# A two-block sequence-mixing kernel on one core: the convolution branch moved to the front of the first block, its taps placed behind the matrix LSTM's projection, and the modulation rows computed in array quadrants

## The reference, cut to what matters

```python
mod_x = split(silu(c) @ w_ada + b_ada, 6);  mod_c = split(silu(c_ctx) @ w_ada + b_ada, 6)
h  = rmsnorm(x, g_norm1) * (1 + mod_x[1]) + mod_x[0]
hc = rmsnorm(ctx, g_norm1) * (1 + mod_c[1]) + mod_c[0]
u_rw, u_cv, u_ml, u_gate = split(h @ w_in)          # RWKV, convolution, matrix LSTM, three merge gates
ya = rwkv_mixer(u_rw, hc @ w_in[rw]); yc = mlstm_mixer(u_ml, hc @ w_in[ml])
a, g = split(u_cv); z = a * sigmoid(g)              # 512 channels each
z = depthwise_conv(z, cv_dw, cv_db)                 # 31 taps, within rows of 64 tokens
yb = silu(layernorm(z, cv_lnw, cv_lnb))
m = sig(ga) * (ya @ p_a) + sig(gb) * (yb @ p_b) + sig(gc) * (yc @ p_c)
x = x + mod_x[2] * (m @ w_out)
x = x + mod_x[5] * mlp(rmsnorm(x, g_norm2) * (1 + mod_x[4]) + mod_x[3])
```

## Time and profile before

| what | value |
|---|---|
| median of 3 runs | 4786.41 us (4783.46 to 4788.29) |
| profiled execution | 4790.0 us, its span 4788.2 us |
| TensorE busy | 4233.6 us (88%) |
| VectorE, ScalarE, GpSimd busy | 2180.8 (46%), 1340.5 (28%), 156.6 us (3%) |
| TensorE's mean granted clock | 0.914 |
| matrix LSTM projection, start to end | 89.8 to 232.4 us |
| RWKV output, from the first slab load | 1029.4 to 1098.4 us |
| convolution projection | 1098.4 to 1146.6 us |
| merge | 1146.6 to 1446.4 us |

### The profile page before, as it was taken

The page is one execution under the profiler, slowest core; times in us unless marked ns, Lnnn a source line. Parts: engine busy times, 40 slices in busy tenths (PEclk is TensorE's granted clock), DMA queues, the critical chain, the costliest instruction groups (busy, mean ns, idle before and its releaser), DMA issues.

```text
span 4788.2 us, 69852 instructions
## 1 busy us (share of the span) xinstructions
PE 4233.6 (88%) x30212; PEld 3338.8 (70%) x30212; DVE 2180.8 (46%) x2940; ACT 1340.5 (28%) x1886; POOL 156.6 (3%) x194
## 2 busy tenths in 40 slices
PE   6987878878677999999987989998999987989998
PEld 3855768856455787788666667887788666567886
DVE  2135467753744444433636344334333636444334
ACT  3133233312122232322221342222222321342222
POOL 0000012120000000000001000000000001000000
PEclk8878979989889999999978989999999978999999
DMA  5101000033123323233200113232333200112331
GB/s 191 45 1 44 9 2 3 3 110 105 53 71 109 117 96 105 80 93 93 71 28 16 40 39 89 85 106 86 95 94 91 63 19 15 40 53 80 97 100 54
DMA packets 319059, 322.10 MB, mean 67 GB/s; under 512 B 10032, under 2 KB 243552, under 8 KB 317984
## 3 DMA queue, kind: packets, MB, share of 16 engines
q1 hardware_dynamic: 312144, 287.53, 19.5%
q0 software_dynamic: 6608, 30.11, 1.7%
HBM read 312.37 MB, written 5.24 MB: 66 GB/s over the span
## 4 chain that ended last, share of the span: by engine, by line
PE 77%; DVE 13%; issue 4%; ACT 4%; DMA 1%; POOL 0%; DVEq 0%; ACTq 0%; POOLq 0%
PE psum L232 76%; DVE ring L286 3%; DVE arena L297 3%; DVE ring L317 2%; DVE arena L286 2%; PE psum L239 1%; ACT arena L336 1%; ACT ring L336 1%; ACT r L336 1%; DVE r L286 1%; DVE arena L293 1%; DMA ring<-in_rw_g 0%; DVE arena L317 0%; DVE arena L291 0%; DVE ring L301 0%
## 5 line engine op out<-in xcount | busy, mean ns | idle before, releaser
L232 PE MATMUL psum<-r 128*128 128x512 f32 (+3 forms) x12912 | 3024.5, 396 | 157.0 <-DVE r L286 141.3
L232 PEld LDWEIGHTS psum<-r 128*128 128x128 f32 (+1 forms) x12912 | 2429.3, 195 | 748.6 <-DVE r L286 90.7
L286 DVE TENSOR_TENSOR r<-ring,r 128x2048 fp32r<-128x2048 f32 (+2 forms) x269 | 580.2, 2157 | 411.6 <-ACT r L336 400.6
L336 ACT ACTIVATE arena<-psum 128x512 f32<-128x512 f32 (+4 forms) x456 | 249.2, 547 | 1306.9 <-PE psum L232 1211.5
L336 ACT ACTIVATE r<-ring 128x2048 fp32r<-128x2048 f32 (+2 forms) x269 | 484.3, 1800 | 417.7 <-PE psum L232 341.1
L232 PE MATMUL psum<-arena 64*64 64x64 f32 (+14 forms) x2384 | 403.9, 337 | 48.7 <-DVE arena L286 17.8
L232 PE MATMUL psum<-ring 64*64 64x64 f32 (+4 forms) x8608 | 352.3, 236 | 84.2 <-ACT ring L336 34.8
L232 PEld LDWEIGHTS psum<-arena 128*128 128x128 f32 (+6 forms) x2384 | 265.2, 187 | 177.4 <-issue 131.7
L232 PEld LDWEIGHTS psum<-ring 64*64 64x64 f32 (+3 forms) x8608 | 290.6, 145 | 125.6 <-issue 47.5
L286 DVE TENSOR_TENSOR arena<-arena,psum 128x512 f32<-128x512 f32 (+2 forms) x192 | 114.9, 598 | 577.2 <-PE psum L232 570.2
L232 PE MATMUL psum<-ring,arena 64*64 64x64 f32 (+6 forms) x2464 | 265.4, 292 | 100.0 <-DVE ring L286 34.5
(11 more groups left out here) (97 smaller groups left out, 1453.0 us busy)
## 6 DMA issues: line engine op xcount, KB each, us to landing
ring<-in_ffa_w_in SPq DMA_DIRECT2D x88, 512.0 KB, 5.2
ring<-in_ffb_w_in SPq DMA_DIRECT2D x88, 512.0 KB, 5.2
ring<-in_w_mlp SPq DMA_DIRECT2D x32, 1024.0 KB, 5.3
ring<-in_w_in SPq DMA_DIRECT2D x31, 1024.0 KB, 5.3
ring<-in_w_ada SPq DMA_DIRECT2D x24, 1024.0 KB, 5.1
ring<-in_mix_w_in SPq DMA_DIRECT2D x24, 1024.0 KB, 5.1
ring<-in_ffa_w_out SPq DMA_DIRECT2D x20, 1024.0 KB, 5.0
ring<-in_ffb_w_out SPq DMA_DIRECT2D x20, 1024.0 KB, 5.0
```

Of the source, the lines that this page charges most:

```text
L232: ins = self.raw.matmul(o, l, r, start=start, stop=stop, skip_group_check=True)
L286: self.done(self.raw and self.raw.tensor_tensor(o, a, b, f), keys)
L336: self.done(self.raw and self.raw.activation(o, i, f, scale=scale, bias=bias), keys)
```

## The change

The convolution's projection comes first, ahead of the matrix LSTM's, with its four slabs in the order a, g, a, g of 256 columns each; the transposes and scaling of the context tiles stand between its second and third slab. The 124 taps are drawn one by one: 10 behind each of the last two convolution slabs, then 9, 14, 22, 22, 22 and the remaining 15 behind the slabs of q, k and v. The sum over taps is spilled to HBM and loaded again behind the RWKV recurrence. The convolution's norm is cut into three steps that stand behind the first three of the six half passes of the merge. The two steps of a modulation row's sum are cut by halves of 64 rows: 16 matmuls of 64 rows for each half part, into two banks and two partition groups, so that four results are added up (ScalarE copies two, VectorE adds two, and a matmul with the table "two" adds the last two while it turns). The opening loads vecs, the identity, x and ctx before the rest of the constants, all squares and the first transposes stand between the modulation parts, and the meeting "normed" is gone. In the RWKV output modulation part 3 stands ahead of the gates, and GpSimd's loads come in another order.

```diff
+    zs = [K.mem[1][:, o - RING:o - RING + 752] for o in (mk + 10544, mk_y, mk_y + 752, mk + 9216)]
+    m.z = [view(x, [94, 8], [1, 94]) for x in zs]
+    m.cacc = m.yaT
...
+    A.top = mk_c + 3008
+    m.cvT = view(al(2048), [512, 4], [1, 512])
...
+    m.csq, m.cmean = view(al(2048), [512, 4], [1, 512]), al(512)
...
+def pe_mod_rows(E, K, part, hf, among=BANKS):
...
+    o, o2 = t.take("mod a", part, hf, among=among), t.take("mod b", part, hf, among=among)
+    for k0 in (0, 4):
+        i, w, _ = t.chunk(K.I["w_ada"], 128 * k0, 4, part * 1024 + 512 * hf, 512, False)
+        for k in range(4):
+            for x in (0, 1):
+                to = 64 * (1 - x if k % 2 else x)
+                keys = [("w used", i)] + ([("mod rows", part, hf)] if k0 else []) if (k, x) == (3, 1) else []
+                t.mm((o2 if k % 2 else o)[to:to + 2, :], m.silcv[HALF[x], k0 + k, :], w[HALF[x], k, :],
+                     k + k0 < 2, k + k0 > 5, *keys)
...
-        t.mm(o[:, 2 * f:2 * f + 2], m.tmp[0:2, 128 * f:128 * f + 128], K.C["ident"][0:2, 0:2], True, True,
+        t.mm(o[:, 2 * f:2 * f + 2], m.tmp[0:66, 128 * f:128 * f + 128], K.V["two"][0:66, 0:2], True, True,
              *([("mod", part)] if f == 7 else []))
...
+def act_mod_rows(a, K, part, hf, last=None):
+    m = K.m
+    a.wait_ge(*K.at("mod zero", part))
...
+    for x in MOD_ROWS:
+        a.copy(m.tmp[x, 512 * hf:512 * hf + 512], K.bank("mod a", part, hf)[x, :], ("mod rows a", part, hf))
+    K.free(a, "mod a", part, hf)
...
+def dve_mod_rows(v, K, part, hf):
+    m = K.m
+    v.wait_ge(*K.at("mod rows a", part, hf))
+    for x in MOD_ROWS:
+        o = m.tmp[x, 512 * hf:512 * hf + 512]
+        v.tt(o, o, K.bank("mod b", part, hf)[x, :], ADD, ("mod rows sb", part))
+    K.free(v, "mod b", part, hf)
...
 def pool_first(E, K):
     g, m = PoolLine(E, "first"), K.m
-    g.load(m.cst, K.I["consts"], "consts")
     g.load(m.vec, K.I["vecs"], "vecs")
+    g.load(m.cst[:, 0:128], K.I["consts"][:, 0:128], "ident")
     for i in range(4):
-        g.load(m.xs[:, 1024 * i:1024 * i + 1024], K.I["x"][0, 128 * i:128 * i + 128, :], "x", i)
...
+    g.load(m.cst[:, 128:], K.I["consts"][:, 128:], "consts")
...
+def pe_first(E, K):
+    t = TensorLine(E, "norm1")
+    for n, (part, hf) in enumerate(MOD1):
+        pe_mod_rows(E, K, part, hf, among=MOD_BANKS)
+        if n == 2:
+            pe_mod_turn(E, K, 0, among=MOD_BANKS)
+            pe_turn(t, K, "n1", range(4), range(4), among=FIRST_BANKS)
+    pe_mod_turn(E, K, 1, among=MOD_BANKS)
+    pe_turn(t, K, "n1", range(4), range(4, 8))
...
+def act_first(E, K):
...
+        squares(i)
+    act_mod_rows(mod, K, 0, 0)
+    act_mod_rows(mod, K, 0, 1)
+    for i in (4, 5):
+        squares(i)
+    act_mod_rows(mod, K, 1, 0, last=0)
+    act_mod_rows(mod, K, 1, 1, last=0)
+    for f in range(8):
+        if f == 1:
+            for _ in range(8):
+                E.ahead()
+        act_turned(a, K, "n1", 512, 0, f)
...
+def dve_first(E, K):
...
+    mod.set(m.tmp[0:66], 0.0, ("mod zero", 0), ("mod zero", 1))
+    for z in m.z:
+        v.set(z, 0.0)
+    for i in range(4):
+        norm(i)
+    dve_mod_rows(mod, K, 0, 0)
+    dve_mod_rows(mod, K, 0, 1)
+    for i in (4, 5):
+        norm(i)
+    dve_mod_rows(mod, K, 1, 0)
+    dve_mod_turn(mod, K, 0)
+    dve_mod_rows(mod, K, 1, 1)
+    dve_mod_turn(mod, K, 1)
+    dve_scale(E, K, m.sc1, 1, "g1")
+    for f in range(8):
+        if f == 1:
+            for _ in range(8):
+                E.ahead()
+        dve_turned(v, K, "n1", 512, 0, f)
...
+def pe_cv_in(E, K):
+    t, m = TensorLine(E, "cv"), K.m
+    for x, half in CV_PARTS:
+        pe_fm(t, K, ("cv", x, half), K.I["w_in"], CVO + 512 * x + 256 * half, 256, 8, m.hL, lambda f: SEGS[0:1],
+              ready="n1")
+        if (x, half) == (1, 0):
+            pe_turn(t, K, "n1c", (4, 5), range(8))
...
+def dve_cv_in(E, K, conv):
+    v, m = VectorLine(E, "cv"), K.m
+    for x, half in CV_PARTS:
+        E.ahead()
+        for f in range(2) if x else ():
+            b = 2 * half + f
+            v.wait_ge(*K.at("cv g sb", half, f))
+            v.tt(m.z[b][:, :, 15:79], h8(K.bank(("cv", 0, half), f, 0)), h8(m.cacc[:, b, :]), MUL, ("cv z", b))
+            K.free(v, ("cv", 0, half), f, 0)
+        if (x, half) == (1, 0):
+            n = VectorLine(E, "norm1")
+            for f in range(8):
+                dve_turned(n, K, "n1c", 256, 1, f)
+        elif half:
+            taps(conv, 10)
...
+def dve_conv(E, K):
+    v, m = VectorLine(E, "cv"), K.m
+    for b in CV_BLOCKS:
+        o, cd = h8(m.cacc[:, b, :]), K.V["cdw"][:, 31 * b:31 * b + 31]
+        v.ts(o, m.z[b][:, :, 0:64], cd[:, 0:1], K.V["cdb"][:, b:b + 1], MUL, ADD)
+        yield
+        for k in range(1, 31):
+            v.stt(o, m.z[b][:, :, k:k + 64], cd[:, k:k + 1], o, MUL, ADD, ("cv taps", b), ("cv acc",))
+            yield
...
+    a.wait_ge(*K.at("cv taps", 3))
...
+    g.wait_ge(*K.at("cv acc"))
+    g.load(K.I["spill"][:, 12:16, :], m.cacc, "spilled cv")
...
+def dve_ml_in(E, K, conv):
     v, m = VectorLine(E, "ml"), K.m
+    for n in range(2):
+        E.ahead()
+        if n == 0:
+            v.wait_ge(*K.at("n1c", "tr", 7))
             v.tt(m.hx1, m.hL[:, 0], m.hL[:, 1], ADD, ("rw hx",))
+        taps(conv, 9 + 5 * n)
+    for _ in range(2):
+        E.ahead()
+        taps(conv, 22)
+    v.wait_ge(*K.at("in", "spilled"))
+    v.set(m.v1[:, :, :, 128:129], 1.0)
+    E.ahead()
+    taps(conv, 22)
+    E.ahead()
+    for _ in conv:
         pass
...
+    for i in range(6):
+        v.wait_ge(*K.at("ml v", 0, i))
+        v.copy(m.v1[:, i, :, 0:128], view(K.bank("ml v", 0, i), [128, 4], [1, 128]), ("ml v1", i))
+        K.free(v, "ml v", 0, i)
...
-    g.load(m.cst[:, m.cst_kept:], K.I["consts"][:, m.cst_kept:], "consts again")
-    g.load(m.ycT, K.I["spill"][:, 8:12, :], "ycT again")
-    g.load(m.hx2, K.I["spill"][:, 0:8, :], "hx")
     g.load(m.g2f, K.I["rw_g2"][0], "g2f")
     g.load(m.lw, row(K.I["rw_lnw"][0, :], 512), "rw_lnw")
     g.load(m.lb, row(K.I["rw_lnb"][0, :], 512), "rw_lnb")
+    g.load(m.hx2, K.I["spill"][:, 0:8, :], "hx")
+    g.load(m.cst[:, m.cst_kept:], K.I["consts"][:, m.cst_kept:], "consts again")
+    g.load(m.ycT, K.I["spill"][:, 8:12, :], "ycT again")
+    g.load(m.cvT, K.I["spill"][:, 12:16, :], "cv again")
...
+    for hf in range(2):
+        dve_mod_rows(mod, K, 3, hf)
     v.wait_ge(*K.at("rw n", "sd"))
...
+    dve_mod_turn(mod, K, 3)
+    dve_mod_rows(mod, K, 4, 0)
+    for i in range(4):
+        y = m.Yb[:, i, :]
         v.wait_ge(*K.at("rw gate", i))
         v.tt(y, y, K.bank("rw gate", i), MUL, ("rw out", i))
         K.free(v, "rw gate", i)
+    dve_mod_rows(mod, K, 4, 1)
     v.wait_ge(*K.at("in", "hx"))
...
+    dve_mod_turn(mod, K, 4)
+    dve_scale(E, K, m.sc2, 4, "g2")
...
+    K.fences[E.slab] = K.late[E.slab] = "RWKV done"
+    pe_mod(E, K, 3)
     t.wait_ge(*K.at("in", "g2f"))
     for i in range(4):
         o = t.take("rw gate", i)
         t.mm(o, m.lo3[:, 2, 128 * i:128 * i + 128], m.g2f, True, True, ("rw gate", i))
-    K.fences[E.slab] = K.late[E.slab] = "RWKV done"
-    for part in (3, 4):
-        pe_mod(E, K, part)
+    pe_mod(E, K, 4)
...
+def pe_column_sums(t, K, name, x, ready):
...
+def act_conv_norm(a, K, step):
...
+        a.wait_ge(*K.at("cv norm"))
+        for f in range(4):
+            a.act(m.cvT[:, f, :], m.cvT[:, f, :], ACT.Silu, scale=K.V["clw"][:, f:f + 1], bias=K.V["clb"][:, f:f + 1])
...
+def dve_conv_norm(v, K, step):
...
+    if step == 0:
+        v.wait_ge(*K.at("cv mean sb"))
+        v.tt(m.cvT, m.cvT, rep(m.cmean, 4, 512), SUB)
+        v.tt(m.csq, m.cvT, m.cvT, MUL, ("cv sq",))
+    elif step == 1:
+        v.wait_ge(*K.at("cv var"))
+        v.ts(m.crs, K.bank("cv var"), 1.0 / 512, 1e-5, MUL, ADD, ("cv rs", "var"))
+        K.free(v, "cv var")
+    else:
+        v.wait_ge(*K.at("cv rs", "sd"))
+        v.recip(m.crs, m.crs)
+        v.tt(m.cvT, m.cvT, rep(m.crs, 4, 512), MUL, ("cv norm",))
...
+MERGE = [(br, pw, hf) for br, pw in BRANCHES for hf in range(2)]
...
+    for n, (br, pw, hf) in enumerate(MERGE):
+        pe_tm(t, K, ("mg gate", br, hf), K.I["w_in"], GO + 1024 * br + 512 * hf, 512, 8, m.hL, W512)
+        if n == 0:
+            pe_column_sums(t, K, "cv mean", m.cvT, ("in", "cv again"))
+        if n == 1:
+            pe_column_sums(t, K, "cv var", m.csq, ("cv sq",))
+        pe_tm(t, K, ("mg y", br, hf), K.I[pw], 512 * hf, 512, 4, m.yop, W512, ready=("yop", br))
...
+            if n:
+                a.wait_ge(*K.at("mg sum", n - 1, i))
...
+            pass
+        if n < 3:
+            act_conv_norm(a, K, n)
...
+            if (n, i) == (0, 0):
+                dve_conv_norm(v, K, 0)
...
+        if n in (1, 2):
+            dve_conv_norm(v, K, n)
...
+    E.wait_ge(*K.at("in", "ident"))
+    pe_first(E, K)
+    pe_cv_in(E, K)
+    pe_ml_in(E, K)
     E.wait_ge(*K.at("in", "consts"))
-    for part in (0, 1):
-        pe_mod(E, K, part)
-    pe_norm1(E, K)
```

(48 more changed lines are left out.)

278 lines of the change are left out of this document (102 added, 176 removed).

## The result

| kernel | median, us | runs | ratio to before, 95% interval |
|---|---|---|---|
| before (beside it, on the same chip) | 4784.93 | 4783.19 to 4788.29 | 1 |
| changed | 4670.14 | 4665.78 to 4679.59 | 0.9762 [0.9745, 0.9779] |

The change gains 114.8 us, 2.4%; 95.4 were forecast (4786.41 to 4691). The time lies inside the range of 4668 to 4716, 2 us above its lower end. The profiled execution took 4665.78 us, its span is 4664.0, and 124.2 less than the 4788.2 of before. (Executions that took over 1.5% longer than the fastest one of the same kernel are left out of all ratios.)

The account below looks back on a forecast made before the run. TensorE was taken as the bound, where nothing keeps it from working; in the merge it waits for VectorE. Terms 39.9 - 48.2 - 6.7 - 80.7 = -95.7 gave 4694.3 us profiled, 4691 median; own range 4678 to 4704, wider range 4668 to 4716.

Parts of the forecast that it names:

- A: Opening and projections, start to last 16-column tile: from 232.43 to 272.3 us, +39.9, with the convolution's projection and taps moved in.
- the 64x64 rows: Profiled matmuls, 35 ns each, read as a floor of overlap; so four quadrants run at once, 1.7 us per modulation slab.
- B: Convolution's projection at its old place, 1098.4 to 1146.6: the stage goes, -48.2 us.
- C: RWKV output: first slabs released by the reloaded constants, stage ends at 1091.7 against 1098.44; -6.7 us, bounds -18 and +3.
- D: Merge: without taps it falls from 299.8 to 219.1 us, -80.7, keeping one 3.7 us wait and 2.5 of low clock.
- Two at a time: Rival for modulation rows: two quadrants run at once, 3.5 us per slab; opening +6, RWKV output +11, 4708; chance 0.16.
- one at a time: Rival for modulation rows: quadrants run singly, 6.9 us per slab; opening +26, RWKV output +38, 4755; chance 0.05.
- slower than before: Rival for modulation rows: quadrants one by one at 1.2 GHz, 13.7 us per slab; +81 and +90, 4862; chance 0.02.
- The merge keeps gaps: Rival in the merge: norm steps hold up ScalarE's roundings; four waits with lost clock, +20 us, 4711; chance 0.08.
- The taps cost less: Rival in the projections: TensorE doesn't stand at the output gate if v's banks free in time; -17, 4674; chance 0.08.

## Why the prediction was right, and where it wasn't

**A (+39.9, measured +36.2; with equal places +37.1 and +40.6).** Right in nearly every step. Slab rows 1.90 us for 1.7, scale at 50.8 for 49.5, the gate at 216.9 for 219.6 after a pause of 14.9 for about 15, last tile 268.6 for 272.3. The pace of the new place (5.49 us per tile instead of 5.60), which I hadn't foreseen, is about 1 us of that: with 8 columns more the last tile comes at 269.6. The eighth slab landed at 42.5, not at 38, and the slabs' rows still ended at 44.7 for 43.6. The reading of the 64x64 rows as a floor of the overlap was right, and two quadrants, tried, cost 3.5 us per slab, as the rival said. The first rows ran at either level of the clock (1.90 and 3.59 us), not at 1.00 as taken for the opening; it cost nothing, as slabs landed later than the rows needed them.

**B (-48.2).** As said.

**C (-6.7, measured +4.5, 11 us short, and outside its upper bound of +3).** This is the step that failed, in two ways. I count from the first slab load. The constants were put down for 18.6 us and TensorE could start at 21.8 (3.2). The fourth slab was asked for at 1083.15, as soon as the first was read, and its rows could start 8.0 us later, where I had allowed 6.1 (1.9): two more slabs were asked for within the next 3.5 us. The stretch of 1058 to 1098 moved 337 GB/s, with a DMA share of 0.90. The larger part, some 6 us, is the clock: 1.9 in the fourth slab's rows, 1.1 up to the end of the turn and 3.0 in the gates. I had charged the lower level to the first two slabs alone, and TensorE stood at it again behind the next waits:

```profile
1091.17:1094.76 3.59, 3.59 (x16) 0.50 0.54 208
1097.52:1101.10 3.58, 3.58 (x17) 0.50 0.50 193
1101.10:1105.10 4.00, 4.00 (x5) 0.50 0.02 4
```

(Length, TensorE busy with its count, granted clock, DMA share, GB/s.) The last slab's rows ended at 58.4 us instead of 47.0; what follows them took 14.6 where 15.3 were forecast. Why the constants came late is open: both kernels moved nearly the same in that time (375 GB/s in 1030 to 1050 of before, 372 in 1058 to 1080 of the changed one, both at a share of 0.97), and before had 4.8 MB of reloads there in 18.5 us, the changed kernel 4.5 MB in 21.6. With the wait moved the stage still takes 66.3 us, 4.5 more than the 61.8 forecast, so the place of that wait is not all of it. An order of loads or a sum of bytes that would bring it down was not tried. In five other kernels with the same order here the stage took 67.8 to 71.7 us, so of the 73.0 some 1 to 5 belong to this execution; where it was shortest (67.8) the fourth slab's rows took 1.90.

**D (-80.7, measured -75.6).** The mechanism held: no wait for taps, a wait of 3.55 (forecast 3.7) in the fourth half pass, two switches of 2.17 (2.2). The merge's tiles kept 2.80 us. What was missing: 1.71 us for the bank of the norm's variance, which VectorE's queue frees late, and the clock. The prediction charged it at the start alone, 2.5. The windows of the changed kernel (the same columns):

```profile
1131.00:1136.00 5.00, 5.00 (x16) 0.71 0.82 266
...
1233.00:1237.00 4.00, 4.00 (x11) 0.59 0.01 4
...
...
1260.70:1265.00 4.30, 4.30 (x13) 0.66 0.76 243
1309.20:1313.00 3.80, 3.80 (x16) 1.00 0.00 0
```

The start costs 5.00 x 0.29 = 1.5, and waits of 2.17 and 3.55 cost 1.6 and 1.5 more each, though the last of 2.17 cost none. 201.6 of matmuls, 6.9 of column sums, 9.6 of waits, 4.6 of clock and about 1 from the last matmul to the last sum make 223.7 of 224.2.

**Behind the merge (0, measured -33.0), and the luck in the sum.** I costed the new table at nothing. Its 32 bytes moved every operand behind it, and that gave back more than C and D had lost. The forecast of 4691 is 21 us too high for this reason alone; with the old places the kernel takes 4704 and would have been 13 us above it. That the time lies in the range is in part luck: C and D fell 16 us short, a term that I had at nothing gave 33, and the sum still passed the lower end by 2.

**Rivals.** Two at a time, one at a time and slower than before are out by 1.90 us per slab; where slabs took 3.4 to 3.6 us, as two at a time would have it, the granted clock was 0.50 to 0.56 in all but the first. "The merge keeps gaps" has a small part of truth, 1.71 and the clock. "The taps cost less" is out as a forecast, and shown as what it would take: v's banks freed in time.

## What to carry to other kernels

Filler work on an engine belongs where that engine isn't the one that feeds TensorE; within such a stretch its last piece still has to stand behind whatever frees banks for the next matmuls. Before a difference of under one per cent is explained by the order of work, compare the pace of one loop that the change doesn't touch: if it differs, pad the layout until it doesn't, and try a few paddings for their own sake. A landing time taken from a trace holds for what was in flight beside it. And where TensorE waits for transfers again and again, price the rows behind each wait at the lower level of the clock, not only the first ones: here that was the larger part of the one step that failed.

## What the runs showed of the hardware

The place of the operands in SBUF changes the pace of the 128x512 matmuls of split products at full granted clock, between 10.99 and 11.20 us per 48 (0.229 and 0.233 each), up to 37 us for the kernel. 32, 64 and 128 bytes from the changed kernel's place gave 4704, 4685 and 4679 us against 4670 (ratios 0.9828, 0.9788 and 0.9794 against 0.9762), and at 128 bytes the tiles of 12 were faster (2.75 for 2.80 us) and those of 48 slower (11.20 for 10.99). Matmuls of 64 rows by 2 columns in all four quadrants ran 3.6 at once, 16 in 1.90 us, with both row halves writing one bank, and 3.5 us with two quadrants; at the lower level of the clock the 16 took 3.59. Waits of only 2.17 and 3.55 us were followed by about 4 us at a mean granted clock of 0.59 and 0.66, but not each of them (the second wait of 2.17 by 1.00). In the RWKV output waits of 4.63 and 2.76 us for a slab and for VectorE stood ahead of rows at 0.50.
